# A long two-block kernel: rounded weights in two slots instead of four, and X kept on chip

## The reference

```python
def _layer(x, c, ...):
    shift, scale, gate = split(c @ w_ada + b_ada, 3)
    h = _rmsnorm(x, norm_g) * (1.0 + scale) + shift
    proj = h @ w_in                                   # 1024 x 4096: eight chunks of 512 columns
    sb_q, sb_k, sb_v, sb_g, df_q, df_k, df_v, df_g = split(proj)
    # stick-breaking attention, 8 heads of 64
    z = sb_q @ sb_k.T * inv
    log_1m = where(mask, log_sigmoid(-z), 0.0)
    rem = reverse_cumsum(log_1m) - log_1m
    sb_out = (where(mask, exp(log_sigmoid(z) + rem), 0.0) @ sb_v) * silu(sb_g)
    # differential attention, 4 heads: two causal softmax maps, their difference times v
    qd, kd = _rmsnorm(df_q, q_norm_g), _rmsnorm(df_k, k_norm_g)
    df_o = (softmax(q1 @ k1.T * inv + bias) - lam * softmax(q2 @ k2.T * inv + bias)) @ df_v
    df_out = _rmsnorm(df_o, subln_g) * (1.0 - lam_init) * silu(df_g)
    out = concat([sb_out, df_out]) @ w_out            # 1024 x 1024: two chunks
    return x + gate * out
```

## Time and profile before

| | |
|---|---|
| median of three runs | 1534.42 us (1534.08 to 1535.58) |
| the profiled execution | 1535.58 us, span of its instructions 1533.6 us |
| TensorE, VectorE, ScalarE, GpSimd busy | 98%, 70%, 45%, 18% of the span |
| granted TensorE clock, mean | 0.999 |
| second block: gate chunk | from 1297.9 us |
| heads 0 to 7 | 1319.8 to 1454.5 us |
| the steps | 1454.5 to about 1490 us |

### The profile page before, as it was taken

How to read it: one execution, slowest core, us unless ns; L and a number is a source line. 1 busy time by engine, 2 the same in 40 slices (tenths; PEclk the granted TensorE clock), 3 DMA queues, 4 the chain that set the end, 5 groups by cost and what they waited for, 6 DMA issues and landing times.

```text
span 1533.6 us, 20882 instructions
## 1 busy us (share of the span) xinstructions
PE 1501.5 (98%) x8203; PEld 1248.3 (81%) x8203; DVE 1066.8 (70%) x1584; ACT 688.9 (45%) x1194; POOL 274.1 (18%) x206
## 2 busy tenths in 40 slices
PE   4999999999999999999999999999999999999999
PEld 3888898888888897977778888888888898877777
DVE  6798688888988773248886685665634653688665
ACT  3433552322314454247775552232314443778761
POOL 0200013233222000048882011111100011010000
PEclk9999999999999999999999999999999999999999
DMA  9675256578576213430000254354423242111211
GB/s 331 248 259 194 83 193 227 198 234 313 199 254 220 77 40 137 137 115 2 2 1 29 83 193 138 117 171 139 163 88 104 83 158 93 55 56 58 87 77 55
DMA packets 109958, 207.53 MB, mean 135 GB/s; under 512 B 6169, under 2 KB 13606, under 8 KB 109862
## 3 DMA queue, kind: packets, MB, share of 16 engines
q1 hardware_dynamic: 109862, 206.21, 39.3%
HBM read 202.00 MB, written 4.19 MB: 134 GB/s over the span
## 4 chain that ended last, share of the span: by engine, by line
PE 84%; DVE 7%; issue 2%; DMA 2%; ACT 2%; POOL 1%; SPq 1%; DVEq 0%; POOLq 0%; ACTq 0%
PE PS L2262 46%; PE PS L2215 23%; DVE MACC L1327 3%; PE PS L2597 3%; PE PS L2624 2%; PE PS L2587 2%; DVE WL L1293 2%; PE PS L2690 1%; PE PS L2286 1%; PE PS L2675 1%; DMA MRAW<-in_ada_w_dram 1%; PE PS L2756 1%; POOL MROW L525 1%; DMA X<-in_x_dram 1%; PE PS L2778 1%
## 5 line engine op out<-in xcount | busy, mean ns | idle before, releaser
L749 ACT ACTIVATE WH<-RAW 128x2048 fp32r<-128x2048 f32 (+1 forms) x105 | 196.8, 1884 | 353.6 <-DMA RAW<-in_ff_w_in_dram 222.9
L1293 DVE TENSOR_TENSOR WL<-RAW,WH 128x2048 fp32r<-128x2048 f32 (+1 forms) x101 | 255.6, 2553 | 76.8 <-ACT WH L749 76.7
L525 POOL PARTITION_ALL_REDUCE MROW<-MACC x26 | 123.3, 4743 | 602.4 <-DVE MACC L1327 515.3
L2262 PE MATMUL PS<-WH,HIDh 128*128 128x512 f32 (+1 forms) x576 | 217.4, 378 | 0.0
L2262 PE MATMUL PS<-WL,HIDh 128*128 128x512 f32 (+1 forms) x576 | 217.3, 377 | 0.0
L2262 PE MATMUL PS<-WH,HIDl 128*128 128x512 f32 (+1 forms) x576 | 217.3, 377 | 0.0
L2262 PE MATMUL PS<-HTh,WH 128*128 128x512 f32 (+1 forms) x520 | 202.5, 389 | 0.6 <-DVE WL L1293 0.6
L2262 PE MATMUL PS<-HTl,WH 128*128 128x512 f32 (+1 forms) x520 | 202.4, 389 | 0.0
L2262 PE MATMUL PS<-HTh,WL 128*128 128x512 f32 (+1 forms) x520 | 202.3, 389 | 0.0
L1327 DVE SCALAR_TENSOR_TENSOR MACC<-MRAW,CS,MACC 128x512 f32<-128x512 f32 x168 | 126.3, 752 | 8.3 <-DMA MRAW<-in_ada_w_dram 0.8
L2262 PEld LDWEIGHTS PS<-WH,HIDh 128*128 128x128 f32 x576 | 108.4, 188 | 20.6 <-issue 0.2
(11 more groups left out here) (361 smaller groups left out, 3035.4 us busy)
## 6 DMA issues: line engine op xcount, KB each, us to landing
MRAW<-in_ada_w_dram SPq DMA_DIRECT2D x44, 1024.0 KB, 7.3
RAW<-in_ff_w_in_dram SPq DMA_DIRECT2D x32, 1024.0 KB, 5.4
RAW<-in_ff_w_out_dram SPq DMA_DIRECT2D x32, 1024.0 KB, 5.1
RAW<-in_w_in_dram SPq DMA_DIRECT2D x16, 1024.0 KB, 5.3
MRAW<-in_w_ada_dram SPq DMA_DIRECT2D x12, 1024.0 KB, 8.6
RAW<-in_a_w_in_dram SPq DMA_DIRECT2D x8, 1024.0 KB, 10.1
MRAW<-in_kv_ada_w_dram SPq DMA_DIRECT2D x8, 1024.0 KB, 6.1
RAW<-in_kv_w_dram SPq DMA_DIRECT2D x6, 1024.0 KB, 5.2
```

Of the source, the lines that this page charges most:

```text
L525: pool.partition_all_reduce(MROW[:], MACC[:], P, RADD).then_inc(m_red, 1)
L749: act.activation(rounded(u)[:, 0:width(u)], RAW[:, u % 4, 0:width(u)], ACT.Copy).then_inc(w_hi, 1)
L1293: dve.tensor_tensor(WL[:, u % 4, 0:width(u)], RAW[:, u % 4, 0:width(u)], rounded(u)[:, 0:width(u)].bitcast(F32), ALU.subtract).then_inc(w_ ...
L2262: mm = pe.matmul(po, a, b_, start=(k == 0 and i == 0), stop=(k == KT - 1 and i == len(ops) - 1), skip_group_check=len(ops) > 3)
```

## The change

WX, x_kept, `over_x`, `rounded` and `next_units` go. `wslot(u)` says that units 98 to 107 use slots 0 and 1 of WH in turn, and all others u % 4 as before. X stays in its place, and the two groups of copies on SyncE and VectorE's wait for the second go. Since unit u now has the slot of u - 2, ScalarE rounds it (`hi_two`) only after TensorE has used u - 2: the first of a chunk after w_used, the second after full, the end of the chunk. Both roundings stand at a chunk's end, in heads 1, 3 and 5, and VectorE's two subtractions behind the two halves of `minus_abs` of the same head. The out chunk's units 108 and 109 are rounded and subtracted in quarters inside the steps. In each head both halves of `sb_log` now come ahead of the first `df_unit`.

```diff
+def wslot(u):
+    return u % 2 if 2 * SG_CHUNK <= u < 2 * OUT_CHUNK else u % 4
...
-        for tt in range(TT):
-            sp.wait_ge(n_x, TT * len(NORM_GROUPS) - TT + tt + 1)
-            sp.dma_start(x_kept[tt * P:(tt + 1) * P, :], X[:, tt, :]).then_inc(x_saved, 16)
...
-        sp.wait_ge(x_saved, 16 * TT)
-        sp.wait_ge(full, 4 * CHUNK_GROUP[OUT_CHUNK - 1] + 4)
-        for tt in range(TT):
-            sp.dma_start(X[:, tt, :], x_kept[tt * P:(tt + 1) * P, :]).then_inc(x_in[tt], 16)
...
-        act.wait_ge(x_saved, 16 * TT)
-        act.wait_ge(n_xn, TT * len(NORM_GROUPS) + TT)
-        chunk(to(lambda b: SV[:, b, :]))
+        def hi_two(u):
+            if u % 2 == 0:
+                act.wait_ge(w_used, u // 2)
+            else:
+                act.wait_ge(full, 4 * CHUNK_GROUP[(u - 3) // 2] + 4)
+            hi(u)
+
+        hi_two(2 * SG_CHUNK)
+        chunk(to(lambda b: SV[:, b, :]), split=False)
+        hi_two(2 * SG_CHUNK + 1)
...
+        def out_hi_quarter(i):
+            u, c_ = 2 * OUT_CHUNK + i // 4, slice(512 * (i % 4), 512 * (i % 4) + 512)
+            if i == 0:
+                act.wait_ge(w_used, OUT_CHUNK)
+            elif i == 4:
+                act.wait_ge(full, 4 * CHUNK_GROUP[OUT_CHUNK - 1] + 4)
+            if i % 4 == 0:
+                act.wait_ge(w_in[u % 4], 16 * (u // 4 + 1))
+            act.activation(WH[:, u % 4, c_], RAW[:, u % 4, c_], ACT.Copy).then_inc(w_hi_out, 1)
...
-        for i in range(2):
-            hi(2 * DF_CHUNK + i)
...
         gate_unit(2)
+        hi_two(2 * DF_CHUNK)
         gate_unit(3)
+        hi_two(2 * DF_CHUNK + 1)
...
-                sb_log(h + 1, 0)
-                df_unit(2 * h)
-                sb_log(h + 1, 1)
+                for part in range(2):
+                    sb_log(h + 1, part)
...
-                df_unit(2 * h)
+            df_unit(2 * h)
...
-            for u in next_units(h):
-                hi(u)
...
+            if h % 2 and h < SB_HEADS - 1:
+                hi_two(2 * DF_CHUNK + h + 1)
             df_unit(2 * h + 1)
...
+            if h % 2 and h < SB_HEADS - 1:
+                hi_two(2 * DF_CHUNK + h + 2)
...
-            if n_ == 13:
+            if n_ <= 8:
+                out_hi_quarter(n_ - 1)
+            elif n_ == 13:
                 df_root(0)
...
                     minus_abs(h + 2, part)
-                if part == 0 and h % 2 and h < SB_HEADS - 1:
-                    for u in next_units(h):
-                        lo(u)
+                if h % 2 and h < SB_HEADS - 1:
+                    lo(2 * DF_CHUNK + h + part + 1)
...
-            if h % 2 == 0:
-                for u in next_units(h):
-                    lo(u)
...
         for n_ in range(1, DF_STEPS - 1):
+            if 3 <= n_ <= 10:
+                out_lo_quarter(n_ - 3)
             difference(n_ + 1)
...
-                dve.wait_ge(x_in[b], 32)
...
-                pe.wait_ge(w_lo, 2 * OUT_CHUNK + 1)
+                pe.wait_ge(w_lo_out, 4)
```

More of the change, by code:

```diff
@@ L82 @@
 SV_CHUNK, SG_CHUNK, DF_CHUNK, OUT_CHUNK = 48, 49, 50, 54
-def over_x(u):
-    return 2 * SG_CHUNK <= u < 2 * OUT_CHUNK and u % 4 >= 2
+def wslot(u):
+    return u % 2 if 2 * SG_CHUNK <= u < 2 * OUT_CHUNK else u % 4
 def freed(group):
@@ L109, in sb @@
         return at(name, shape, dt, offset), offset
-    X, o_x = sb("X", [P, TT, D])
+    X, _ = sb("X", [P, TT, D])
     Y, o_y = sb("Y", [P, TT, D])
@@ L228, in program @@
     PS = nc.alloc_psum_tensor("PS", [P, 8, 512], F32)
-    x_kept = nc.dram_tensor("x_kept", (T, D), F32, kind="Internal").ap()
-    def rounded(u):
-        return WX[:, u % 2, :] if over_x(u) else WH[:, u % 4, :]
     def sem(name):
@@ L748, in hi @@
             act.wait_ge(w_in[u % 4], 16 * (u // 4 + 1))
-            act.activation(rounded(u)[:, 0:width(u)], RAW[:, u % 4, 0:width(u)], ACT.Copy).then_inc(w_hi, 1)
+            act.activation(WH[:, wslot(u), 0:width(u)], RAW[:, u % 4, 0:width(u)], ACT.Copy).then_inc(w_hi, 1)
         def split_next():
@@ L1290, in lo @@
         def lo(u, at_=None):
-            dve.wait_ge(w_hi, at_ or u + 1)
+            dve.wait_ge(w_hi, at_ or (u - 1 if u > 2 * OUT_CHUNK else u + 1))
             dve.tensor_tensor(WL[:, u % 4, 0:width(u)], RAW[:, u % 4, 0:width(u)],
-                              rounded(u)[:, 0:width(u)].bitcast(F32), ALU.subtract).then_inc(w_lo, 1)
+                              WH[:, wslot(u), 0:width(u)].bitcast(F32), ALU.subtract).then_inc(w_lo, 1)
         def lo_half(u, i):
@@ L2009, in recip, with out_lo_quarter @@
             dve.reciprocal(r, r).then_inc(d_rc, 1)
+        def out_lo_quarter(i):
+            u, c_ = 2 * OUT_CHUNK + i // 4, slice(512 * (i % 4), 512 * (i % 4) + 512)
+            dve.wait_ge(w_hi_out, i + 1)
+            dve.tensor_tensor(WL[:, u % 4, c_], RAW[:, u % 4, c_], WH[:, u % 4, c_].bitcast(F32), ALU.subtract
+                              ).then_inc(w_lo_out, 1)
         def gated_weight(i, part, parts):
@@ L2207, in three @@
             o = 512 * (k % 4)
-            h, l = rounded(u)[:, o:o + 512], WL[:, u % 4, o:o + 512]
+            h, l = WH[:, wslot(u), o:o + 512], WL[:, u % 4, o:o + 512]
             ah, al = th[:, k, :], tl[:, k, :]
@@ L2241, in chunk @@
                 o = width * (k % 4)
-                h, l = rounded(u)[:, o:o + width], WL[:, u % 4, o:o + width]
+                h, l = WH[:, wslot(u), o:o + width], WL[:, u % 4, o:o + width]
                 ah, al = (early if early is not None and k < 4 else (th, tl))
@@ L2862, in pe_program @@
         out_first(3).then_inc(w_used, 1)
-        pe.wait_ge(w_lo, 2 * OUT_CHUNK + 2)
+        pe.wait_ge(w_lo_out, 8)
         n.tile += 8
```

8 lines of the change are left out of this document (2 added, 6 removed).

## The result

The kernel after the change takes 1543.26 us (median of 4 runs, 1542.74 to 1544.16), the kernel before 1534.25 (1533.44 to 1535.58) on the same chip. The ratio is 1.0064, with a 95% interval of 1.0051 to 1.0078: 9.0 us slower. The forecast was 1544.0, and 1545.2 for a profiled execution; that took 1545.44, with a span of 1543.5. Five more executions of the kernel after took 1543.18 to 1545.88, so all ten lie within 3.1 us; their median is 1544.56.

The account below looks back on a forecast made before the run. TensorE was taken as the bound, busy 1501.5 of 1533.6 us. Terms 1.55 + 0.1 + 3.25 + 2.41 + 1.10 + 1.2 = 9.6 us moved the median from 1534.42 to 1544.0; range 1539.5 to 1547.5.

Parts of the forecast that it names:

- Gate chunk to head 0: Head 0: a rounding ahead of the table load and both logs ahead of the eviction delay TensorE's second product by 1.55 us.
- Head 1, evictions and first wait of the boundary: Head 1: swapped logs cost 0.1 us; TensorE's wait for subtraction 102, behind half of minus_abs, costs 2.45 us.
- Second wait of that boundary: Boundary in head 1: TensorE waits 0.80 us for subtraction 103, behind the second half of minus_abs.
- Head 3: Boundary in head 3: TensorE waits 1.63 us for subtraction 104 and 0.78 for 105, together 2.41 us.
- Head 5: Boundary in head 5: TensorE waits 0.31 us for subtraction 106 and 0.79 for 107, together 1.10 us.
- Steps: Differential-attention steps: quarters of steps 4 and 8, ahead of DT copies, cost 0.55 us each; 1.2 us together.
- The waits on WL: Sign: TensorE waits for VectorE's subtractions six or seven times, near 7 us in all, the longest 2.4 in head 1.
- A: Rival: two slots suffice, roundings and subtractions slip into gaps, only the steps' 1.2 us remains; 1535.6, no change; chance 0.07.
- B: Rival: faster; lighter heads 6 and 7 and spared traffic remove 1.5 us of waits, quarters cost nothing; 1532.9; chance 0.02.
- C: Rival: the quarters in the steps find no cover, +4.4 us instead of 1.2; 1547.2; chance 0.08.
- D: Rival: clock falls; 12 slow matmuls behind each of three waits of 1.5 us or more add 8.6 us; 1552.6; chance 0.05.
- ScalarE's slip of 1.8 us: Heads 1, 3, 5: table load and next head's weights slip 1.8 us, at no cost because TensorE is 1.1 to 3.3 later.

Follow-up runs that it names:

- logs_back: Kernel after, with the first differential eviction of a head again between the two logs, as before the change: 1544.11 us, ratio 1.0060.
- no_wl_no_hi: Kernel after, subtractions of units 102 to 107 and second roundings of units 101, 103, 105, 107 cut to 16 of 2048 columns: 1536.23 us, ratio 1.0014.
- again: Kernel after, run once more unchanged: 1543.54 us, ratio 1.0059.
- no_quarters: Kernel after, with the quarter roundings and subtractions of units 108 and 109 left out of the steps: 1543.66 us, ratio 1.0055.
- quarters_moved: Kernel after, with the quarters of steps 4 and 8 moved behind the DT and DO of steps 5 and 9: 1544.13 us, ratio 1.0063.
- no_wl: Kernel after, with the subtractions of units 102 to 107 cut to 16 of 2048 columns and TensorE reading WH instead: 1541.26 us, ratio 1.0038.

## Why the prediction was right

It was right by its steps, with one of them too small, one reason that is right at one place of two, and one that holds only by accident. Against the stretch of the kernel after:

- *Gate chunk to head 0:* 1.55 predicted, 1.44 measured (column 0). logs_back gives 0.5 of it to the logs. That the rest is the rounding ahead of the table load is borne out by no_wl_no_hi, where the column is at 16.25 with the changed order of logs.
- *Head 1, evictions and first wait of the boundary:* 0.1 + 2.45 predicted, 2.47 measured (column 1).
- *Second wait of that boundary:* 0.80 predicted. Column 2 has 1.67 with the clock fall and 0.82 without (again). The step as put, a wait, is right where the clock holds. In the profiled execution TensorE worked at half its clock until the second subtraction was done and had no wait left.
- *Head 3:* 2.41 predicted, 1.63 + 0.83 = 2.46 measured. *Head 5:* 1.10 predicted, 0.31 + 0.82 = 1.13 measured.
- *Steps:* 1.2 predicted, 1.11 measured (0.51 up to the first DT copy that TensorE waits for, 0.59 from there to the second), and no_quarters gives back 1.07. The place is as said. The reason, that just the two quarters ahead of those copies cost and the others find cover, is right at the first copy only: at the second, quarters_moved takes the one ahead of it away and gains nothing.

The sum of the terms was 9.6. It is 9.5 where the clock holds (212.04 - 202.55) and 10.3 where it falls. That the median came out at 9.0 has luck in it, with executions that spread by 3 us.

**The signs.** The waits on WL were to be six or seven, near 7 us in all and 2.4 at most; they are five, 4.7 and 2.2 (six and 5.1 in again), and that on DSQ is 1.0 instead of 1.5. The list counts TensorE's idle time from the end of the matmul before, while the prediction took differences of starts: by starts the boundaries cost 6.9 us in again, where 6.8 and 0.1 for the evictions were forecast. The period of the steps is 9.51 (9.6 predicted), and the heads grew by 8.4 in again and 9.2 in the kernel after (8.4 predicted). One sign against the forecast did appear: matmuls 0.63 us long behind a wait, in head 1.

**The rivals.** A and B fall with the waits on WL. C falls with column "to out". D, given 0.05 and priced at 8.6, was half right: the clock can fall behind a wait in a busy stretch, but of the three waits only the longest did it, it cost 0.8 to 0.9 us and not 2.9, and it did not come in every execution. The trace of before had an instance near 685 us, in a stretch with more waits, which the prediction did not use; with it 0.05 was low. The price failed in its assumption of 12 slow matmuls (there are eight) that all count: half of their cost lies in the time that TensorE would have waited for the second subtraction anyway (8 x 0.20 = 1.6 us slower, of which the 0.8 of the second wait had to be spent either way). As a part of the forecast's own range, not as a rival of its own, it would have been placed better.

**The reason that holds by accident.** The prediction let ScalarE's slip of 1.8 us in heads 1, 3 and 5 go at nothing, since TensorE would be later by then too. That is true, but it made the three terms look as if they belonged to VectorE's subtractions, and they do not belong to them alone: without those subtractions only 2.9 of 9.5 us come back (no_wl), and 5.1 more when the second roundings go too (no_wl_no_hi). Two late chains run side by side, and the sum shows only the later one. Of the 10.29 us of the changed kernel, taken off in this order, 0.80 are the clock, 2.88 the subtractions, 5.10 the second roundings (head 0's among them), 1.07 the quarters and 0.28 the order of the logs; 0.16 are left (10.29 - 10.13). In another order the shares would be others: with the roundings and logs untouched the subtractions are worth 2.9, while the waits' list puts 4.7 us on them.

Open is why the clock held in one execution of five with the same wait in head 1, and in six of thirteen near 685 us, and where the 2.1 us of spread ahead of 676 us come from; no experiment went there. Nor was a longer wait tried.
